# Expert stage: normalised rows stored k-major, and the slot table turned round between the two down steps

## The chip, the cores and the metric

The kernel runs on one core of one Trainium2 chip. The metric is the device time of one execution in microseconds (us); the times below are medians of a few executions. The engines are named as in the profile: PE is TensorE (PEld its weight loads), DVE is VectorE, ACT is ScalarE, POOL is GpSimd, SP is SyncE, which here only issues DMAs.

## The reference, cut to what matters

Two transformer blocks over 256 tokens of width 2048. The change touches only the mixture of experts in the first one, and the normalised rows that feed it:

```python
def hierarchical_moe(hn, w_router_group, w_router_expert, w_gate, w_up, w_down):
    """hn: (B,S,D). Top-1 group, then top-2 experts in that group; SwiGLU experts."""
    ...
    ids = g_idx * EXPERTS_PER_GROUP + top_i
    comb = jnp.sum(jax.nn.one_hot(ids, N_EXPERTS, dtype=jnp.float32) * weights[..., None], axis=1)
    out = jnp.zeros((b * s, d), jnp.float32)
    for e in range(N_EXPERTS):
        hid = jax.nn.silu(t @ w_gate[e]) * (t @ w_up[e])
        out = out + (hid @ w_down[e]).astype(jnp.float32) * comb[:, e:e + 1]
```

There are 32 experts with a hidden width of 256. All weights are float32, so the expert stage has to read 32 x 3 x 2048 x 256 x 4 bytes, 201 MB.

## The kernel before

Everything is written engine by engine, with semaphores by hand; the order on each engine is the order of the code.

**Rows.** POOL multiplies the normalised rows `hs` by the gain `g_row` and writes `xs` (L532, one instruction for each of the two token tiles of 128). ACT copies `xs` to `x_hi` in TensorE's rounded format (L1334), DVE makes `x_lo = xs - x_hi` (L1886). Behind these stand, on ACT the copy of the router's logits `lgT` (L1336), on DVE the whole routing, which ends with the one-hot slot table `G` (token by 64 slots for each expert, L1964), and on PE the product for `w_ple_up` and the ranks of the tokens.

**Gather.** The experts are worked off in 16 pairs. A gather (L901) makes two of the 16 k-tiles of the transposed rows `xg` for two pairs at once: 8 matmuls of 128x128 weights, which are columns of `x_hi` or `x_lo`, by 256 columns of `g_quad`, a copy of a piece of `G`. Feature number q*16 + k is row q of k-tile k, because the expert weights are read as `"e (p k) n -> e p (k n)"` so that each partition reads one piece of memory. So the weights of a gather are every 16th element of a row, 64 bytes apart, by the view `x_k` at L589. Eight gathers run ahead of the stage, and four in each of the pairs 0 to 13.

**One pair g.** PE runs `gate_up(g, 0..3)` (L951, into `ps`), `transpose(g)`, `down(g, 0..1)` (L973, into `acc`), and four `move(g, q)` between them. A move is a scatter of pair g-1, a gather and a second scatter. A scatter (L913, L914) brings the results `yh`, `yl` of pair g-1 back to the token rows by the turned slot table `GT`; DVE adds them to `h` (L2003). `transpose(g)` turns the hidden rows `hid` (L922) into the left half of a buffer `tp` and the pair's part of `G` (L924) into its right half; ACT copies the halves to `hid_t` (L1380) and `GT` (L1381) and then frees the buffer.

**Buffers.** All of moves and transposes go through two `tp` buffers in turn (`use`, L887): a use waits on `t_read[b]` until ACT or DVE has read the use before the last one.

**Weights.** SP loads them in 6 steps for each pair, each of 2 MB in two or four DMAs, into a ring of 4 steps (`load_step`, L413); a step's DMAs are issued when PE has used the step four before.

**Overflow.** Tokens beyond an expert's 64 slots are handled by a branch after the stage (`xT`, `ov_w`), which no instruction of the profile shows as run.

Of the kernel before, what the change touches and what calls it, by code (L numbers as in the profile page):

```python
# [27 lines left out]
P = 128  # L28
# [72 lines left out]
def program(nc, I, out):  # L101
    ctx = ExitStack()
    with ctx:
# [199 lines left out]
        silu_ready, hid_ready, hid_lo = sem("silu_ready"), sem("hid_ready"), sem("hid_lo")  # L303
# [29 lines left out]
        def _(sp):  # L333
# [60 lines left out]
            wg = I["w_expert_gate"][0].rearrange("e (ko p) n -> p (e ko) n", p=P)  # L394
            wu = I["w_expert_up"][0].rearrange("e (ko p) n -> p (e ko) n", p=P)
# [36 lines left out]
            with sp.If(count > 0):  # L432
                with sp.Fori(0, count) as i:
                    ex = sp.value_load(over_i[0:1, bass.ds(i + 1, 1)], min_val=0, max_val=N_EXPERTS - 1)
                    sp.wait_ge(ov_pe, i * OV_PE + OV_X)
                    sp.dma_start(ov_w[:, :, :], wg[:, bass.ds(ex * KT, KT), :]).then_inc(ov_in, 16)
                    sp.wait_ge(ov_pe, i * OV_PE + (OV_X + 1))
                    sp.dma_start(ov_w[:, :, :], wu[:, bass.ds(ex * KT, KT), :]).then_inc(ov_in, 16)
# [56 lines left out]
        def _(pool):  # L495
# [93 lines left out]
        x_k = [x.rearrange("p t (q k) -> p t k q", k=KT) for x in (x_hi, x_lo)]  # L589
        USES = 8 + 8 * PAIRS + 4 * (PAIRS - 2) + PAIRS + 1  # L590
# [7 lines left out]
        def _(pe):  # L598
# [285 lines left out]
            gathered = []  # L884
# [22 lines left out]
            def scatter(g, k):  # L907

                pe.wait_ge(y_ready, 2 * g + k // 4 + 1)
                o = use()  # L910
                q = slice(k % 2 * P, k % 2 * P + P)
                cs = slice(k // 2 * 512, k // 2 * 512 + 512)
                pe.matmul(o[:, :], GT[:, g % 2, q], yh[:, cs], start=True, stop=False, skip_group_check=True)  # L913
                pe.matmul(o[:, :], GT[:, g % 2, q], yl[:, cs], start=False, stop=True, skip_group_check=True).then_inc(t_done, 1)  # L914

            def transpose(g):

                pe.wait_ge(hid_ready, g + 1)
                o = use()
                hid_j = hid[:, g % 2, :].rearrange("p (q j) -> p j q", j=2)  # L920
# [35 lines left out]
            def down(g, j):  # L956
# [33 lines left out]
            for g in range(PAIRS):  # L990
# [11 lines left out]
                down(g, 0)  # L1002
                down(g, 1)
# [8 lines left out]
            with pe.If(count > 0):  # L1012
                for k in range(KT // 2):
                    if k >= 2:
                        pe.wait_ge(ov_act, k - 1)
                    for j in range(2):
                        f = slice((2 * k + j) * P, (2 * k + j + 1) * P)
                        for t in range(TT):
                            pe.matmul(tp[k % 2][:, j * S + t * P:j * S + (t + 1) * P], x_hi[:, t, f], ident_r[:, :],
                                      start=True, stop=False, skip_group_check=True)  # L1020
                            mm = pe.matmul(tp[k % 2][:, j * S + t * P:j * S + (t + 1) * P], x_lo[:, t, f], ident_r[:, :],
                                           start=False, stop=True, skip_group_check=True)
# [121 lines left out]
        def _(act):  # L1144
# [187 lines left out]
            for t in range(TT):  # L1332
                act.wait_ge(xs_ready, t + 1)
                act.activation(x_hi[:, t, :], xs[:, t, :], ACT.Copy).then_inc(xh_ready, 1)  # L1334
# [41 lines left out]
            def transposed(g):  # L1376
# [3 lines left out]
                act.activation(hid_t[:, :, :].rearrange("p a b -> p (a b)"), tp[b][:, 0:S], ACT.Copy).then_inc(hid_lo, 1)  # L1380
                act.activation(GT[:, g % 2, :], tp[b][:, S:2 * S], ACT.Copy).then_inc(t_read[b], 1)  # L1381
# [16 lines left out]
            for g in range(PAIRS):  # L1398
# [12 lines left out]
                moved(g, 3)  # L1411
                if g % 2 and g // 2 + 2 < PAIRS // 2:
# [117 lines left out]
        def _(dve):  # L1530
# [353 lines left out]
            for t in range(TT):  # L1884
                dve.wait_ge(xh_ready, t + 1)
                dve.tensor_tensor(x_lo[:, t, :], xs[:, t, :], x_hi[:, t, :], ALU.subtract).then_inc(xl_ready, 1)  # L1886
# [150 lines left out]
            for g in range(PAIRS):  # L2037
# [10 lines left out]
                moved(g, 3)  # L2048
            evict(PAIRS - 1)
# [300 lines left out]
```

## Time and profile before

| | us |
|---|---|
| three runs | 2441.45, 2442.82, 2431.88; median 2441.45 |
| the profiled execution | 2437.95 |
| its span in the trace | 2436.1 |
| PE busy | 2290.0 (94%) |
| DVE, ACT, POOL busy | 1339.8, 902.1, 25.6 |
| expert stage with its first gathers, in the span | 454.35 to about 1005 |
| PE's granted clock, mean | 0.977 of full speed |

Busy time of an engine isn't the time that it sets: what matters is which engine or transfer the others wait for in a stage. Durations are read in the stage that the change touches; matmuls are pipelined, so that the distance between starts tells more than the length of one.

### The profile page before, as it was taken

What the parts mean: (1) busy time and instruction counts of PE and PEld (TensorE: products, weight loads), DVE (VectorE), ACT (ScalarE), POOL (GpSimd) and SP (SyncE); (2) the same over time, 40 slices, a digit from 0 to 9 for tenths busy, and PEclk for the clock granted to TensorE, in tenths of its full rate; (3) what the DMA queues carried; (4) which work ended last, traced back from release to release, by engine and by line L of the source; (5) the groups of instructions that cost most, each with busy time, mean ns of one, the idle gap of its engine ahead of it and who ended that gap; (6) DMA issues with size and microseconds to landing.
All of it is one profiled execution on the core that took longest, in us unless ns stands there. A gap on an engine that the chain in (4) does not pass through costs nothing.

```text
span 2436.1 us, 31362 instructions
## 1 busy us (share of the span) xinstructions
PE 2290.0 (94%) x11443; PEld 1745.5 (72%) x11443; DVE 1339.8 (55%) x1760; ACT 902.1 (37%) x1197; POOL 25.6 (1%) x32
## 2 busy tenths in 40 slices
PE   8999789899999999898999869989999999999997
PEld 7888567654554444487888647867888888878886
DVE  7679845322222222555555557656777777764443
ACT  4464344311111111344333355444443344343332
POOL 1000000100000000000000000000000000000000
PEclk9999999999999999899999999999999999999998
DMA  8655335499999999566656505544655665556663
GB/s 286 183 161 155 104 127 194 166 358 368 374 391 372 368 363 401 208 192 215 190 190 191 155 18 160 179 128 142 187 185 186 185 185 187 183 183 195 192 194 126
DMA packets 301285, 519.26 MB, mean 213 GB/s; under 512 B 24032, under 2 KB 196096, under 8 KB 292224
## 3 DMA queue, kind: packets, MB, share of 16 engines
q1 hardware_dynamic: 298272, 505.51, 61.3%
q0 software_dynamic: 2912, 12.38, 1.5%
q8 instruction: 66, 1.08, 0.2%
q14 instruction: 35, 0.29, 0.0%
HBM read 515.67 MB, written 5.27 MB: 214 GB/s over the span
## 4 chain that ended last, share of the span: by engine, by line
PE 88%; DVE 7%; ACT 2%; issue 1%; DMA 1%; POOL 0%; DVEq 0%; SPq 0%; ACTq 0%; POOLq 0%
PE acc L610 27%; PE acc L630 24%; PE acc L631 12%; PE ps L951 9%; PE tp L901 5%; PE acc L973 5%; PE tp L913 1%; DVE rst L1838 1%; PE tp L914 1%; PE tp L686 1%; DVE wlo L1543 1%; DVE e L1702 1%; DVE sneg L1679 1%; PE tp L766 1%; DMA mw<-in_w_expert_up 1%
## 5 line engine op out<-in xcount | busy, mean ns | idle before, releaser
L630 PE MATMUL acc<-xhl,whi 128*128 128x512 f32 x2496 | 888.1, 401 | 13.9 <-DVE rxp L1595 6.5
L1159 ACT ACTIVATE whi<-raw 128x1024 fp32r<-128x1024 f32 x572 | 587.6, 1055 | 547.5 <-DMA raw<-in_w_in 186.1
L1543 DVE TENSOR_TENSOR wlo<-raw,whi 128x1024 fp32r<-128x1024 f32 x572 | 673.2, 1220 | 207.7 <-ACT whi L1159 203.9
L631 PE MATMUL acc<-xhl,wlo 128*128 128x256 f32 x2496 | 702.2, 281 | 0.0
L630 PEld LDWEIGHTS acc<-xhl,whi 128*128 128x128 f32 x2496 | 472.4, 189 | 132.0 <-DVE rxp L1595 7.2
L631 PEld LDWEIGHTS acc<-xhl,wlo 128*128 128x128 f32 x2496 | 474.5, 190 | 0.1
L610 PE MATMUL acc<-whi,xhl 128*128 128x512 f32 x1248 | 400.1, 397 | 13.5 <-DVE wlo L1543 10.3
L610 PEld LDWEIGHTS acc<-whi,xhl 128*128 128x128 f32 x1248 | 236.3, 189 | 68.0 <-DVE wlo L1543 13.2
L610 PE MATMUL acc<-wlo,xhl 128*128 128x512 f32 x624 | 244.7, 392 | 0.0
L951 PE MATMUL ps<-mw,xg 128*64 128x512 f32 x1024 | 229.8, 595 | 1.6 <-DMA mw<-in_w_expert_up 0.9
L2003 DVE TENSOR_TENSOR h<-tp,h 128x512 f32<-128x512 f32 x128 | 87.8, 690 | 207.0 <-PE tp L914 206.4
L951 PEld LDWEIGHTS ps<-mw,xg 128*64 128x64 f32 x1024 | 70.9, 137 | 140.5 <-issue 137.7
L610 PEld LDWEIGHTS acc<-wlo,xhl 128*128 128x128 f32 x624 | 118.4, 190 | 26.5 <-issue 2.6
L610 PE MATMUL acc<-whi,ah 128*128 128x512 f32 x336 | 131.8, 392 | 4.3 <-DVE xhl L2233 4.3
L610 PE MATMUL acc<-wlo,ah 128*128 128x512 f32 x336 | 131.7, 392 | 0.0
L610 PE MATMUL acc<-whi,al 128*128 128x512 f32 x336 | 131.5, 391 | 0.0
L1364 ACT ACTIVATE xg<-tp 128x512 f32<-128x512 f32 x64 | 38.2, 597 | 246.6 <-PE tp L901 246.6
L973 PE MATMUL acc<-mw,hid_t 128*64 128x512 f32 x512 | 113.5, 596 | 0.0
L2024 DVE SCALAR_TENSOR_TENSOR yl<-acc,w_slot,yh 128x1024 fp32r<-128x1024 f32 x32 | 39.6, 1279 | 123.9 <-ACT yh L1373 123.9
L973 PEld LDWEIGHTS acc<-mw,hid_t 128*64 128x64 f32 x512 | 35.4, 137 | 69.8 <-issue 69.8
L901 PE MATMUL tp<-g_quad,x_hi 128*128 128x256 f32 x256 | 75.8, 379 | 8.0 <-ACT g_quad L1358 7.1
L901 PEld LDWEIGHTS tp<-g_quad,x_hi 128*128 128x128 f32 x256 | 68.3, 309 | 18.0 <-issue 9.6
(343 smaller groups left out, 1867.4 us busy)
## 6 DMA issues: line engine op xcount, KB each, us to landing
raw<-in_w_in SPq DMA_DIRECT2D x352, 256.0 KB, 3.0
raw<-in_w_up SPq DMA_DIRECT2D x352, 256.0 KB, 2.9
mw<-in_w_expert_gate SPq DMA_DIRECT2D x128, 512.0 KB, 7.2
mw<-in_w_expert_up SPq DMA_DIRECT2D x128, 512.0 KB, 8.1
mw<-in_w_expert_down SPq DMA_DIRECT2D x64, 1024.0 KB, 11.0
raw<-in_w_down SPq DMA_DIRECT2D x176, 256.0 KB, 3.4
raw<-in_w_out SPq DMA_DIRECT2D x128, 256.0 KB, 3.3
raw<-in_w_ple_gate SPq DMA_DIRECT2D x64, 256.0 KB, 3.5
```

Of the source, the lines that this page charges most:

```text
L610: mm = pe.matmul(o, lhsT, rhs, start=first and j == 0, stop=last and j == 2, skip_group_check=True)
L630: pe.matmul(o.rearrange("p (m n) -> p m n", m=2), wh, ahl[:, :, k, :], start=first, stop=False, skip_group_check=True)
L631: return pe.matmul(o[:, S:2 * S], wl, ahl[:, 0, k, :], start=False, stop=last, skip_group_check=True)
L686: mm = pe.transpose(tp[g % 2][:, j * S + t * P:j * S + t * P + P], src[:, t, f], ident[:, :])
L901: mm = pe.matmul(o[:, j * 2 * P:(j + 1) * 2 * P], x_k[m // TT][:, m % TT, 2 * k + j, :], g_quad[:, q % 2, m % TT, :], start=m == 0, stop=m ...
L951: mm = pe.matmul(ps[g % 2][r, :].rearrange("p (a n) -> p a n", a=2), x_e, mw[:, s0 + 2 * e:s0 + 2 * e + 2, k * 256:(k + 1) * 256], start=c ...
L973: mm = pe.matmul(acc[c][r, n5], hid_t[:, j, r], mw[:, s0 + 2 * e + c, n5], start=j == 0, stop=j == 1, skip_group_check=True)
L1159: act.activation(whi[:, m % RING, :], raw[:, m % RING, :], ACT.Copy).then_inc(hi_ready, 1)
L1364: act.activation(xg[:, q % 2, 2 * k:2 * k + 2, :].rearrange("p a b -> p (a b)"), tp[b][:, :], ACT.Copy).then_inc(t_read[b], 1)
L1543: dve.tensor_tensor(wlo[:, m % RING, :], raw[:, m % RING, :], whi[:, m % RING, :], ALU.subtract).then_inc(lo_ready, 1)
L2003: dve.tensor_tensor(hh, tp[b][:, :], hh, ALU.add).then_inc(t_read[b], 1)
L2024: dve.scalar_tensor_tensor(yl[:, cs], acc[b][:, :], w_slot[:, g:g + 1], yh[:, cs], ALU.mult, ALU.subtract).then_inc(y_ready, 1)
```

## The change

`xs`, `x_hi` and `x_lo` are stored in the order k, q: the 128 elements of one k-tile lie side by side. POOL reads as before and writes 512 bytes apart. The copies of ACT and DVE take the new shape, whole rows as before. The gather's weights are now contiguous. Since the overflow branch shares these rows, its order of features changes with them, and so do the views of its weights.

The turning of the slot table leaves `transpose(g)` and gets a function and a `tp` use of its own, `slots_back(g)`, between `down(g, 0)` and `down(g, 1)`. The semaphore `hid_lo` goes; `down(g, 0)` waits on the `t_read` of `transpose(g)`'s buffer, and the first scatter of pair g on that of `slots_back(g)`. ACT copies `GT` behind the fourth gather's `xg`.

```diff
-        xs = at("xs", 33, [P, TT, D])
-        x_lo = at("x_lo", 33, [P, TT, D], F32R)
-        x_hi = at("x_hi", 49, [P, TT, D], F32R)
+        xs = at("xs", 33, [P, TT, KT, P])
+        x_lo = at("x_lo", 33, [P, TT, KT, P], F32R)
+        x_hi = at("x_hi", 49, [P, TT, KT, P], F32R)
...
-                pool.tensor_tensor(xs[:, t, :], hs[:, t, :], g_row[:, :], ALU.mult).then_inc(xs_ready, 1)
+                pool.tensor_tensor(xs[:, t, :, :].rearrange("p k q -> p q k"), hs[:, t, :].rearrange("p (q k) -> p q k", k=KT),
+                                   g_row.rearrange("p (q k) -> p q k", k=KT), ALU.mult).then_inc(xs_ready, 1)
...
-        x_k = [x.rearrange("p t (q k) -> p t k q", k=KT) for x in (x_hi, x_lo)]
-        USES = 8 + 8 * PAIRS + 4 * (PAIRS - 2) + PAIRS + 1
+        x_k = [x_hi, x_lo]
+        USES = 8 + 8 * PAIRS + 4 * (PAIRS - 2) + 2 * PAIRS + 1
...
                 pe.wait_ge(y_ready, 2 * g + k // 4 + 1)
+                if k == 0:
+                    pe.wait_ge(t_read[back_use[g] % 2], back_use[g] // 2 + 1)
                 o = use()
...
                 for j in range(2):
-                    pe.transpose(o[:, j * P:(j + 1) * P], hid_j[:, j, :], ident[:, :])
+                    mm = pe.transpose(o[:, j * P:(j + 1) * P], hid_j[:, j, :], ident[:, :])
+                mm.then_inc(t_done, 1)
+
+            def slots_back(g):
+
+                o = use()
+                back_use.append(tu.n - 1)
                 for t in range(TT):
-                    mm = pe.matmul(o[:, S + t * P:S + (t + 1) * P], G[:, t, pair_cols(g)], ident_b[:, :], start=True,
+                    mm = pe.matmul(o[:, t * P:(t + 1) * P], G[:, t, pair_cols(g)], ident_b[:, :], start=True,
                                    stop=True, skip_group_check=True)
                 mm.then_inc(t_done, 1)
...
                 if j == 0:
-                    pe.wait_ge(hid_lo, g + 1)
+                    pe.wait_ge(t_read[hid_use[g] % 2], hid_use[g] // 2 + 1)
...
                 move(g, 3)
                 down(g, 0)
+                slots_back(g)
                 down(g, 1)
...
-                act.activation(hid_t[:, :, :].rearrange("p a b -> p (a b)"), tp[b][:, 0:S], ACT.Copy).then_inc(hid_lo, 1)
-                act.activation(GT[:, g % 2, :], tp[b][:, S:2 * S], ACT.Copy).then_inc(t_read[b], 1)
+                act.activation(hid_t[:, :, :].rearrange("p a b -> p (a b)"), tp[b][:, 0:S], ACT.Copy).then_inc(t_read[b], 1)
+                tu.n += 1
+
+            def slots_back(g):
+
+                b = tu.n % 2
+                act.wait_ge(t_done, tu.n + 1)
+                act.activation(GT[:, g % 2, :], tp[b][:, 0:S], ACT.Copy).then_inc(t_read[b], 1)
                 tu.n += 1
```

PE before, pair 1 from its transposes to the second down step (`tp0` and `tp1` are the two buffers; what a row waits for stands in brackets):

```order
L922 MATMUL tp1<-ident,hid_130 128x128 [waits t_read1,hid_ready]
L922 MATMUL tp1<-ident,hid_130 128x128
L924 MATMUL tp1<-ident_b_110,G_115 128x128 x2
L913 MATMUL tp0<-yh_127,GT_116 128x512 [waits t_read0,y_ready]
L914 MATMUL tp0<-yl_128,GT_116 128x512
L901 MATMUL tp1<-g_quad_107,x_hi_106 128x256 [waits t_read1]
...
L913 MATMUL tp0<-yh_127,GT_116 128x512 [waits t_read0,y_ready]
L914 MATMUL tp0<-yl_128,GT_116 128x512
L973 MATMUL acc0<-mw_52,hid_t_131 64x512 [waits w_in_g2,y_ready,hid_lo]
L973 MATMUL acc0<-mw_52,hid_t_131 64x512 x3
L973 MATMUL acc1<-mw_52,hid_t_131 64x512 x4
L973 MATMUL acc0<-mw_52,hid_t_131 64x512 [waits w_in_g3]
```

PE after the change, the same stretch of a pair (the line numbers are those of the changed kernel: L902 is the gather, L916 and L917 the scatter, L926 the transposes, L934 the slot table, L983 the down step):

```order
L926 MATMUL tp0<-ident,hid_130 128x128 [waits t_read0,hid_ready]
L926 MATMUL tp0<-ident,hid_130 128x128
L916 MATMUL tp1<-yh_127,GT_116 128x512 [waits t_read1,y_ready]
L917 MATMUL tp1<-yl_128,GT_116 128x512
L902 MATMUL tp0<-g_quad_107,x_hi_106 128x256 [waits t_read0]
...
L983 MATMUL acc0<-mw_52,hid_t_131 64x512 [waits w_in_g0,y_ready,t_read0]
L983 MATMUL acc0<-mw_52,hid_t_131 64x512 x3
L983 MATMUL acc1<-mw_52,hid_t_131 64x512 x4
L934 MATMUL tp0<-ident_b_110,G_115 128x128 [waits t_read0]
L934 MATMUL tp0<-ident_b_110,G_115 128x128
L983 MATMUL acc0<-mw_52,hid_t_131 64x512 [waits w_in_g1]
```

The two matmuls of the slot table moved from between the transposes and a scatter into the middle of the down steps, and wait there for a buffer.

ACT before, from the third gather of a pair to the results `yh` of the same pair:

```order
L1364 ACTIVATE xg_54<-tp0 128x512 [waits t_done]
L1380 ACTIVATE hid_t_131<-tp0 128x256 [waits t_done]
L1381 ACTIVATE GT_116<-tp0 128x256
L1364 ACTIVATE xg_54<-tp0 128x512 [waits t_done]
L1373 ACTIVATE yh_127<-acc0,w_slot_122 128x1024 [waits w_used,w_ready]
```

and after:

```order
L1374 ACTIVATE xg_54<-tp0 128x512 [waits t_done]
L1390 ACTIVATE hid_t_131<-tp0 128x256 [waits t_done]
L1374 ACTIVATE xg_54<-tp0 128x512 [waits t_done]
L1397 ACTIVATE GT_116<-tp0 128x256 [waits t_done]
L1383 ACTIVATE yh_127<-acc0,w_slot_122 128x1024 [waits w_used,w_ready]
```

The copy of `GT` went behind the fourth gather's copy and has a wait of its own; on DVE nothing moves.

## Rows read from the trace of the kernel before

**Rows 1.** Windows: us, busy of PE, PEld, DVE, ACT, POOL, granted clock, DMA share, GB/s.
```profile
450.00:460.00 10.00, 5.66 (x25) 5.69 (x26) 5.87 (x16) 2.35 (x4) 0.00 (x0) 0.66 0.93 373
...
500.00:940.00 440.00, 435.02 (x1938) 216.69 (x1936) 108.38 (x143) 75.75 (x124) 0.00 (x0) 1.00 0.95 375
945.00:996.00 51.00, 47.66 (x206) 17.09 (x202) 13.63 (x20) 5.29 (x10) 0.00 (x0) 1.00 1.02 410
```

**Rows 2.** The line of the gather: duration ns min/median/max, first and last start.
```profile
L901 PEld LDWEIGHTS tp<-g_quad,x_hi x256: 291/314/331, 454.3 to 931.0; 128*128 128x128 f32 x128
```

**Rows 3.** Timeline, router product, contiguous weights: start us, us, engine line op, count.
```profile
430.66 0.39 PE L610 MATMUL ps<-xhl,rt_hi 128*128 128x256 f32 x2
...
433.12 0.28 PE L610 MATMUL ps<-xhl,rt_hi 128*128 128x256 f32 x1
...
430.77 0.19 PEld L610 LDWEIGHTS ps<-xhl,rt_lo 128*128 128x128 f32 x1
```

**Rows 4.** Timeline, end of pair 7: third move, transposes, fourth move.
```profile
723.51 0.19 PEld L913 LDWEIGHTS tp<-yh,GT 128*128 128x128 f32 x1 [0.81 <-issue]
...
724.08 0.50 PE L901 MATMUL tp<-g_quad,x_hi 128*128 128x256 f32 x2
724.38 0.68 DVE L2003 TENSOR_TENSOR h<-tp,h 128x512 f32<-128x512 f32 x1
...
725.75 0.39 PE L913 MATMUL tp<-yh,GT 128*128 128x512 f32 x1
...
726.41 0.69 DVE L2003 TENSOR_TENSOR h<-tp,h 128x512 f32<-128x512 f32 x1 [1.34 <-PE tp L914]
726.69 0.47 PE L922 MATMUL tp<-ident,hid 128*128 128x128 f32 x2 [0.32 <-ACT xg L1364]
727.00 0.27 PE L924 MATMUL tp<-ident_b,G 128*128 128x128 bf16 x2
727.25 0.47 PE L913 MATMUL tp<-yh,GT 128*128 128x512 f32 x1
...
728.02 0.51 PEld L901 LDWEIGHTS tp<-g_quad,x_hi 128*128 128x128 f32 x2 [0.51 <-ACT GT L1381]
...
729.90 0.40 PE L913 MATMUL tp<-yh,GT 128*128 128x512 f32 x1
...
730.47 0.65 PE L973 MATMUL acc<-mw,hid_t 128*64 128x512 f32 x2
```

**Rows 5.** Timeline, second move of pair 7, PE and DVE.
```profile
717.70 0.50 PE L901 MATMUL tp<-g_quad,x_hi 128*128 128x256 f32 x2
717.90 0.69 DVE L2003 TENSOR_TENSOR h<-tp,h 128x512 f32<-128x512 f32 x1 [3.56 <-PE tp L914]
...
719.36 0.40 PE L913 MATMUL tp<-yh,GT 128*128 128x512 f32 x1
```

**Rows 6.** The chain of waits ahead of the stage, in order of time: start us, us, what.
```profile
423.50 10.02 POOL xs L532 x2
433.54 1.91 ACT x_hi L1334
...
454.35 14.55 PE tp L901 x64
```

**Rows 7.** Timeline, matmuls of the first gathers.
```profile
454.93 0.66 PE L901 MATMUL tp<-g_quad,x_lo 128*128 128x256 f32 x2
...
458.06 0.60 PE L901 MATMUL tp<-g_quad,x_hi 128*128 128x256 f32 x2
...
459.40 0.61 PE L901 MATMUL tp<-g_quad,x_lo 128*128 128x256 f32 x2
```

**Rows 8.** Timeline of the loads of a step and of PE in pair 15.
```profile
473.31 4.26 SPq L413 DMA_DIRECT2D mw<-in_w_expert_down  x4
...
975.27 3.65 PE L951 MATMUL ps<-mw,xg 128*64 128x512 f32 x16 [0.34 <-DMA mw<-in_w_expert_up]
980.37 3.65 PE L951 MATMUL ps<-mw,xg 128*64 128x512 f32 x16 [0.32 <-DMA mw<-in_w_expert_up]
```

More of the change, by code:

```diff
@@ L302, in program @@
                                                                  ("rt_in", "rt_split", "rt_mm", "rt_copy", "rt_tp", "rt_read", "rt_e"))
-        silu_ready, hid_ready, hid_lo = sem("silu_ready"), sem("hid_ready"), sem("hid_lo")
+        silu_ready, hid_ready = sem("silu_ready"), sem("hid_ready")
         moe_in, xs_ready, xh_ready, xl_ready, quad_ready = (sem(n) for n in (
@@ L392, in _ @@
                 load(k2(w_pu, 0, slice(c * 512, c * 512 + 512)))
-            wg = I["w_expert_gate"][0].rearrange("e (ko p) n -> p (e ko) n", p=P)
-            wu = I["w_expert_up"][0].rearrange("e (ko p) n -> p (e ko) n", p=P)
+            wg = I["w_expert_gate"][0].rearrange("e (p k) n -> p e (k n)", p=P)
+            wu = I["w_expert_up"][0].rearrange("e (p k) n -> p e (k n)", p=P)
             wd = I["w_expert_down"][0].rearrange("e (ko p) n -> p (e ko) n", p=P)
@@ L435, in _ @@
                     sp.wait_ge(ov_pe, i * OV_PE + OV_X)
-                    sp.dma_start(ov_w[:, :, :], wg[:, bass.ds(ex * KT, KT), :]).then_inc(ov_in, 16)
+                    sp.dma_start(ov_w.rearrange("p a b -> p (a b)").unsqueeze(1), wg[:, bass.ds(ex, 1), :]).then_inc(ov_in, 16)
                     sp.wait_ge(ov_pe, i * OV_PE + (OV_X + 1))
-                    sp.dma_start(ov_w[:, :, :], wu[:, bass.ds(ex * KT, KT), :]).then_inc(ov_in, 16)
+                    sp.dma_start(ov_w.rearrange("p a b -> p (a b)").unsqueeze(1), wu[:, bass.ds(ex, 1), :]).then_inc(ov_in, 16)
                     sp.wait_ge(ov_pe, i * OV_PE + (OV_X + 2))
@@ L883, in _ @@
             tu = Count()
-            gathered = []
+            gathered, hid_use, back_use = [], [], []
             def use():
@@ L919, in transpose @@
                 o = use()
+                hid_use.append(tu.n - 1)
                 hid_j = hid[:, g % 2, :].rearrange("p (q j) -> p j q", j=2)
                 for j in range(2):
-                    pe.transpose(o[:, j * P:(j + 1) * P], hid_j[:, j, :], ident[:, :])
+                    mm = pe.transpose(o[:, j * P:(j + 1) * P], hid_j[:, j, :], ident[:, :])
[3 more added lines that the diff above has]
+                back_use.append(tu.n - 1)
                 for t in range(TT):
-                    mm = pe.matmul(o[:, S + t * P:S + (t + 1) * P], G[:, t, pair_cols(g)], ident_b[:, :], start=True,
+                    mm = pe.matmul(o[:, t * P:(t + 1) * P], G[:, t, pair_cols(g)], ident_b[:, :], start=True,
                                    stop=True, skip_group_check=True)
@@ L1016, in _ @@
                     for j in range(2):
-                        f = slice((2 * k + j) * P, (2 * k + j + 1) * P)
                         for t in range(TT):
-                            pe.matmul(tp[k % 2][:, j * S + t * P:j * S + (t + 1) * P], x_hi[:, t, f], ident_r[:, :],
+                            pe.matmul(tp[k % 2][:, j * S + t * P:j * S + (t + 1) * P], x_hi[:, t, 2 * k + j, :], ident_r[:, :],
                                       start=True, stop=False, skip_group_check=True)
-                            mm = pe.matmul(tp[k % 2][:, j * S + t * P:j * S + (t + 1) * P], x_lo[:, t, f], ident_r[:, :],
+                            mm = pe.matmul(tp[k % 2][:, j * S + t * P:j * S + (t + 1) * P], x_lo[:, t, 2 * k + j, :], ident_r[:, :],
                                            start=False, stop=True, skip_group_check=True)
@@ L1333, in _ @@
                 act.wait_ge(xs_ready, t + 1)
-                act.activation(x_hi[:, t, :], xs[:, t, :], ACT.Copy).then_inc(xh_ready, 1)
+                act.activation(x_hi[:, t, :, :], xs[:, t, :, :], ACT.Copy).then_inc(xh_ready, 1)
             act.wait_ge(rt_mm, 1)
@@ L1411, in _ @@
                 moved(g, 3)
+                slots_back(g)
                 if g % 2 and g // 2 + 2 < PAIRS // 2:
@@ L1885, in _ @@
                 dve.wait_ge(xh_ready, t + 1)
-                dve.tensor_tensor(x_lo[:, t, :], xs[:, t, :], x_hi[:, t, :], ALU.subtract).then_inc(xl_ready, 1)
+                dve.tensor_tensor(x_lo[:, t, :, :], xs[:, t, :, :], x_hi[:, t, :, :], ALU.subtract).then_inc(xl_ready, 1)
             dve.wait_ge(rt_tp, 1)
@@ L2048, in _ @@
                 moved(g, 3)
+                tu.n += 1
             evict(PAIRS - 1)
```

## The prediction, made before the changed kernel ran

> **What bounds the kernel now.** I read four views, in this order. The windows of the expert stage say that PE is busy for 435.0 of 440 us at full granted clock, and that the DMA engines are busy for 0.95 of it as well [rows 1]. So PE sets the pace of the pairs 1 to 13, but the DMA follows closely. A pair needs 12.58 MB, and at the 375 GB/s of that window this is 33.55 us a pair; in the trace the same row returns every 33.63 us. In a stretch where the DMA is never idle it moves 410 GB/s [rows 1], which is 5.11 us for a step of 2.1 MB and 30.7 us for a pair: no change to PE can bring a pair below that. Next, the gather's line against another product with the same shape. The gather's weight load takes a median of 314 ns [rows 2]; the router's, which also loads 128x128 float32 but from contiguous memory, takes 190 ns [rows 3]. What counts is the distance between starts: six gather matmuls take 1.34 us from 458.06 to 459.40, 0.223 us each [rows 7], the router's 21 matmuls from 430.66 to 433.12 take 0.117 us each [rows 3], with the same 256 moving columns. So the gather is paced by its weight loads and the router by its columns. Third, the timeline of the moves shows who waits for whom around the gathers [rows 4, 5]. Last, the chain of waits ahead of the stage: POOL's two products, ACT's copy and then PE stand in it one behind the other [rows 6].
>
> **The storage order: the gathers.** The only thing about the gather's matmuls that changes is the distance of the weight elements, 64 bytes before and 4 after. I price it by the router's row, which differs in nothing that the rows show: a matmul falls from 0.223 to 0.117 us, and a gather of eight from 1.66 us (717.70 to 719.36, [rows 5]) to 0.94 us. The other bound is no gain at all (a rival below).
>
> How much of the 0.72 us reaches the end is decided by the two buffers. The second scatter of a move writes the buffer of the first, so it waits until DVE has read that one. In the second move DVE reads until 718.59, 0.89 us after the gather's start, and a handover from DVE to PE takes some 0.12 us (727.10 to the weight load ahead of 727.25, [rows 4]): 1.01 us, a little more than the shorter gather. Now DVE is early and hidden behind the gather; it will be late by 0.07 us. So the first and the second move gain 1.66 - 1.01 = 0.65 us each.
>
> The third move, the transposes and the fourth move go together, since a wait in one eats what the one before gained [rows 4]. First scatter at 723.51 as now; gather from 724.08 to 725.02. DVE reads that scatter late, until 725.06, as it made `hid` first; second scatter at 725.18 instead of 725.75. The transposes follow the gather's end by ACT's copy, 0.94 us (725.75 to 726.69): 725.96. The fourth move's first scatter needs DVE's read of the scatter before, 1.50 us after that one's start (725.75 to 727.25): 726.68. That is later than the end of the transposes even without the slot table, so taking the table's two matmuls (0.27 us) out of there gains nothing by itself: the wait on DVE takes their place. Gather 0.57 us later, at 727.25; second scatter 1.01 us behind it, 728.26; down step 0.57 us behind that (729.90 to 730.47), at 728.83. It starts at 730.47 now: gain 1.64 us. The 0.51 us in which the fourth gather waits for ACT's `GT` copy is in this sum; it goes, as `hid_t` alone is read long before 727.25.
>
> **The slot table's new place.** Two bf16 matmuls, 0.27 us, between down steps that use half the array each. The buffer is free: ACT has read the fourth gather's `xg` while `down(g, 0)` runs for 3.5 us. Changing between half and full array costs too. Bounds: 0.27 us, and 0.27 + 0.81 us, the idle time of the weight load at the nearest such change [rows 4], most of which lies beside running matmuls. I take 0.5 us. The second down step, SP's release of its ring slot and ACT's `yh` wait behind it, by 0.5 us. ACT's `GT` copy (0.38 us) lies beside the second down step and is needed 10 us later. The first scatter's new wait is met by then.
>
> A pair gains 2 x 0.65 + 1.64 - 0.5 = 2.44 us, and the 13 pairs with four gathers and scatters 31.7 us. Their new period is 31.2 us, 0.5 us above the DMA's 30.7.
>
> **First gathers, pairs 0, 14, 15.** The first eight gathers, 64 matmuls, take 14.55 us on the chain [rows 6]. PE was idle ahead of them, and the granted clock is 0.66 of full over 450 to 460 us [rows 1], the lower level at first: rows start 0.45 us apart from 454.93 on and last 0.66 us, at 458.06 they last 0.60 [rows 7]. At half clock 256 columns take about twice the router's 0.117 us, so the first 15 matmuls gain nothing. The other 49 gain 0.106 us each, 5.2 us. ACT's copies of 0.6 us keep up with a gather in 0.94. Pair 0 has four gathers without scatters, the last behind many small matmuls; I count three at 0.85 us less 0.5 for the slot table, 2.0 us. Pairs 14 and 15 have no gathers, pay 0.5 and get back the wait for `GT`: 0.
>
> **The storage order: POOL.** POOL's two products are 10.02 us of the chain [rows 6]: x_hi, the logits, the ranks and the slot table all wait behind them, and what they grow by, the kernel grows by. They read as before and write 512 bytes apart. No row has a strided write on POOL. Bounds: 0, if reading two operands sets its pace, and +10 us, if a strided write doubles it (the nearest row of a stride is PE's load, 314 against 190 ns, 1.65 times, which would be +6.5). I take 0, since only one of three operands changed, and keep +10 for the range. ACT's and DVE's passes over the rows stay whole and contiguous: 0.
>
> On this the Trainium skill speaks against the change. GPSIMD Engine Reference, "Performance pitfalls for Q7 kernels", says that reading with a step above 8 bytes costs about half more per element; it says nothing on writes. If writes paid the same, the sum would be 5 us worse, about 2406. No row here shows it.
>
> **DMA.** With pairs of 31.2 us the DMA is busy for 0.98 of the time and its lead is thinner when pairs 14 and 15, which PE does in some 27 us, come. Already now pair 15 waits for weights, 0.3 us at a time [rows 8]. I count 2 us (0 to 6). In all, the ring's first slot comes free at about 468 (473.31 [rows 8] less 5.2), and 92 steps of 5.11 us end near 940, before PE's own last down step at about 956, so the floor isn't reached as a whole.
>
> HBM Reference, "Specifications (TRN2)", gives a core 358 GB/s when both cores of a pair stream and about 425 alone. By 358 the stage would be bound by the DMA today and gain nothing; by 425 the 2 us would go. The rows, 375 over 440 us and 410 over 51 us, speak for the second.
>
> **Sum.** 5.2 + 2.0 + 31.7 - 2 = 36.9 us off the profiled execution's 2437.95 (span 2436.1 and 1.9 around it): 2401. That execution lies between the three runs, 3.5 us below their median and 6 above the lowest, so 2401 stands for a middling run.
>
> **Rivals.** (a) *The DMA becomes the bound.* If, when loaded without a break, it keeps only what the long window implies, 375 / 0.95 = 395 GB/s, a pair takes 31.9 us instead of 31.2: 9 us for 13 pairs, and some 2 more at the end, 2412. For it: its share is at 0.95 already. Against it: 410 over 51 us. (b) *POOL's strided write is late*: +5 to +10 us, 2406 to 2411. (c) *The loads aren't slow because of the stride*, so the change doesn't do what it says: the gathers stay, 16 x 0.5 us come on, up to 0.5 us of `GT` waits for each pair go: 2437 to 2446, taken 2442. Against it: the router's loads. (d) *Slower*: POOL writes each element of the strided output on its own. From a pass of 29.5 us instead of 5.0 on (14 ns an element against 2.4 now) the gain is gone and 12 us lost: 2450 and more. Only the lack of any row speaks for it. (e) Handovers shrink more than I count, or the slot table costs 0.3: 2391.
>
> **How the numbers follow.** Forecast (2394 to 2407) 0.59, (a) 0.13, (b) 0.17, (c) 0.05, (d) 0.02, (e) 0.04. The likeliest gives 2401. The range 2391 to 2413 takes in the forecast, (a), (b) and (e) and leaves out (c), (d) and the ends of the spread. A measurement of this kernel can tell about 0.5% (12 us) from no change. Faster by more than that: 0.93; within: 0.05, from (c) and the far end of (b); slower: 0.02, from (d).
>
> **What would show it.** The gather's weight load near 190 ns and its matmuls 0.117 us apart; moves one and two with the second scatter released by DVE; a pair every 31.2 us; the first gathers done in about 9.4 us; POOL's two products still 10 us; DMA share near 0.98, and PE's waits for weights below 10 us in all. Weight loads still at 314 ns would make the prediction wrong by its whole size; PE waiting for weights in every pair would speak for (a); a longer POOL row for (b).

## The result, and the profile after

| | us |
|---|---|
| after, four runs | median 2396.57 (2394.19 to 2399.26) |
| before, four runs | median 2436.66 (2431.79 to 2442.82) |
| after / before | 0.983, 95% interval 0.980 to 0.987 |
| the profiled execution after | 2394.19, its span 2392.4 |
| forecast | 2401, range 2391 to 2413 |

The change saves 40 us of the medians, 1.7%, and 43.8 us between the two profiled executions. The forecast was 4 us too high. Line numbers are those of the changed kernel from here on: L902 is the gather, L916 and L917 the scatter, L926 the transposes, L934 the slot table, L961 gate_up, L983 the down step, and DVE's addition to `h` is L2020.

First the stage as a whole, to be laid beside [rows 1]. The windows of the kernel after, with the same columns:

```profile
450.00:460.00 10.00, 5.95 (x37) 5.98 (x38) 5.58 (x16) 3.28 (x6) 0.00 (x0) 0.66 0.92 356
500.00:900.00 400.00, 394.57 (x1890) 175.40 (x1888) 105.96 (x141) 74.64 (x121) 0.00 (x0) 1.00 1.01 402
```

In 400 us PE is still busy for 394.6 us, but the DMA share has risen from 0.95 to 1.01 and the rate from 377 (the kernel before over the same 400 us; 375 over the 440 us of [rows 1]) to 402 GB/s. Next, the gather's line (duration in ns min/median/max, first and last start), the answer to [rows 2]:

```profile
L902 PEld LDWEIGHTS tp<-g_quad,x_hi x256: 186/188/338, 454.0 to 894.2; 128*128 128x128 f32 x128
L902 PE MATMUL tp<-g_quad,x_hi x256: 274/282/582, 454.1 to 894.3; 128*128 128x256 f32 x128
```

The weight load fell from 314 to 188 ns, that of the router's contiguous load [rows 3]. The chain of waits ahead of the stage, as in [rows 6], and the line of POOL's products in full:

```profile
423.16 10.07 POOL xs L532 x2
433.25 1.91 ACT x_hi L1344
...
454.05 9.40 PE tp L902 x64
```

```profile
L532 POOL TENSOR_TENSOR xs<-hs,g_row x2: 4627/5051/5475, 423.2 to 428.6; 128x2048 f32<-128x2048 f32 x2
```

POOL writes 512 bytes apart and takes 10.07 us for both products, against 10.02 before. The first gathers take 9.40 us instead of 14.55 (in other executions with the same loads 9.4 to 10.1, by how long the lower clock lasts). Their timeline shows the two clock levels, the answer to [rows 7]:

```profile
456.75 0.63 PE L902 MATMUL tp<-g_quad,x_hi 128*128 128x256 f32 x2
...
457.55 0.40 PE L902 MATMUL tp<-g_quad,x_hi 128*128 128x256 f32 x2
457.79 0.40 PE L902 MATMUL tp<-g_quad,x_lo 128*128 128x256 f32 x2
```

Rows of two start 0.43 us apart until 457.18, which is the lower clock, and 0.24 us apart from 457.55 on, 0.12 us a matmul.

Last, the timeline of one pair, the second move and then the stretch of [rows 4]:

```profile
695.83 0.50 PE L916 MATMUL tp<-yh,GT 128*128 128x512 f32 x1
...
696.41 0.40 PE L902 MATMUL tp<-g_quad,x_hi 128*128 128x256 f32 x2
...
696.61 0.69 DVE L2020 TENSOR_TENSOR h<-tp,h 128x512 f32<-128x512 f32 x1 [3.57 <-PE tp L917]
...
697.42 0.19 PEld L916 LDWEIGHTS tp<-yh,GT 128*128 128x128 f32 x1
697.45 0.47 PE L916 MATMUL tp<-yh,GT 128*128 128x512 f32 x1
...
698.08 3.65 PE L961 MATMUL ps<-mw,xg 128*64 128x512 f32 x16
...
701.67 0.50 PE L916 MATMUL tp<-yh,GT 128*128 128x512 f32 x1
...
704.13 0.48 PE L926 MATMUL tp<-ident,hid 128*128 128x128 f32 x2
...
704.95 0.47 PE L916 MATMUL tp<-yh,GT 128*128 128x512 f32 x1 [0.34 <-DVE h L2020]
...
705.49 0.39 PE L902 MATMUL tp<-g_quad,x_hi 128*128 128x256 f32 x2
...
706.53 0.47 PE L916 MATMUL tp<-yh,GT 128*128 128x512 f32 x1
...
707.15 3.65 PE L983 MATMUL acc<-mw,hid_t 128*64 128x512 f32 x16
...
710.73 0.11 PEld L934 LDWEIGHTS tp<-ident_b,G 128*128 128x128 bf16 x2 [0.81 <-issue]
...
710.95 3.65 PE L983 MATMUL acc<-mw,hid_t 128*64 128x512 f32 x16
...
714.44 1.03 PE L961 MATMUL ps<-mw,xg 128*64 128x512 f32 x4
```

By the spacing of its matmuls the gather is over at about 697.36, and DVE's read ends at 697.30; the second scatter starts at 697.45, 1.04 us after the gather's start (forecast 1.01). In the fourth move the first scatter waits for DVE, as forecast. To measure the same stretches before, four more rows of the kernel before are wanted: the start of the second move, the weight load of its second scatter and the gate_up behind it (around [rows 5]), and the gate_up behind the down steps of [rows 4]:

```profile
717.12 0.50 PE L913 MATMUL tp<-yh,GT 128*128 128x512 f32 x1
...
719.23 0.20 PEld L913 LDWEIGHTS tp<-yh,GT 128*128 128x128 f32 x1
...
719.92 3.65 PE L951 MATMUL ps<-mw,xg 128*64 128x512 f32 x16
...
737.39 3.17 PE L951 MATMUL ps<-mw,xg 128*64 128x512 f32 x14
```

The move took 2.80 us and takes 2.25 now (695.83 to 698.08). The two down steps took 6.92 us (730.47 [rows 4] to 737.39) and take 7.29 with the slot table in between (707.15 to 714.44).

What the stage gained in all is read further down: the second group of transposes in the code behind it (L686 before, L687 after, in the chain that ended last) starts at 980.91 instead of 1018.46, 37.55 us earlier. The forecast's sum was 36.9.

### The profile page after: what moved, and what is told of

Same layout as the page of the kernel before. It is cut to its first block, busy times and chain, and to the rows that moved or that the text cites. A ratio compares the mean times of both kernels' runs of the same rounds, so it can differ in the third digit from the quotient of the medians.

```text
span 2392.4 us, 31362 instructions
## 1 busy us (share of the span) xinstructions
PE 2245.1 (94%) x11443; PEld 1697.4 (71%) x11443; DVE 1340.0 (56%) x1760; ACT 904.3 (38%) x1197; POOL 25.7 (1%) x32
## 4 chain that ended last, share of the span: by engine, by line
PE 89%; DVE 7%; ACT 2%; issue 1%; DMA 1%; POOL 0%; DVEq 0%; SPq 0%; ACTq 0%; POOLq 0%
PE acc L611 27%; PE acc L631 25%; PE acc L632 13%; PE ps L961 9%; PE acc L983 5%; PE tp L902 3%; PE tp L916 2%; PE tp L917 1%; DVE rst L1855 1%; PE tp L687 1%; DVE e L1719 1%; DVE sneg L1696 1%; PE tp L767 1%; DVE h L2020 1%; DVE wlo L1560 1%
## 5 line engine op out<-in xcount | busy, mean ns | idle before, releaser
L961 PE MATMUL ps<-mw,xg 128*64 128x512 f32 x1024 | 229.7, 595 | 1.4 <-issue 0.7
L2020 DVE TENSOR_TENSOR h<-tp,h 128x512 f32<-128x512 f32 x128 | 87.6, 690 | 171.9 <-PE tp L917 171.9
L961 PEld LDWEIGHTS ps<-mw,xg 128*64 128x64 f32 x1024 | 70.9, 137 | 140.2 <-issue 137.5
L983 PE MATMUL acc<-mw,hid_t 128*64 128x512 f32 x512 | 117.6, 601 | 0.0
L983 PEld LDWEIGHTS acc<-mw,hid_t 128*64 128x64 f32 x512 | 34.1, 137 | 62.6 <-issue 61.0
L1521 ACT ACTIVATE ah<-af 128x512 f32 (+1 forms) x21 | 13.3, 632 | 170.5 <-DVE af L2249 170.5
L611 PEld LDWEIGHTS acc<-whi,ah 128*128 128x128 f32 x336 | 63.5, 189 | 17.8 <-DVE xhl L2251 4.6
```

Of the source, the lines that this page charges most:

```text
L611: mm = pe.matmul(o, lhsT, rhs, start=first and j == 0, stop=last and j == 2, skip_group_check=True)
L961: mm = pe.matmul(ps[g % 2][r, :].rearrange("p (a n) -> p a n", a=2), x_e, mw[:, s0 + 2 * e:s0 + 2 * e + 2, k * 256:(k + 1) * 256], start=c ...
L983: mm = pe.matmul(acc[c][r, n5], hid_t[:, j, r], mw[:, s0 + 2 * e + c, n5], start=j == 0, stop=j == 1, skip_group_check=True)
L2020: dve.tensor_tensor(hh, tp[b][:, :], hh, ALU.add).then_inc(t_read[b], 1)
```

## The experiments

A good measure of the stage is the period: the distance between the transposes of neighbouring pairs in the timeline, which repeats within 0.07 us through pairs 1 to 13 in every kernel but e10_short_gate; the table has its mean. The one beside it is the time from the transposes of pair 0 to those of pair 15. Total times of single executions scatter by some 15 us (17 runs of the kernel before, beside the first four kernels: 2426.32 to 2441.64), too much for terms of 5 us; the periods don't.

| kernel | time, us | period | pair 0 to 15 | DMA share, GB/s, 500 to 900 |
|---|---|---|---|---|
| before | 2436.66 | 33.64 | 493.6 | 0.95, 377 |
| after | 2396.57 | 31.38 | 464.7 | 1.01, 402 |
| after_again | 2397.03 | 31.38 | 464.7 | 1.01, 402 |
| e1_order_alone | 2391.65 | 31.03 | 461.1 | 1.01, 406 |
| e2_slots_alone | 2439.48 | 33.63 | 495.2 | 0.95, 377 |
| e7_slots_in_ps | 2388.19 | 31.01 | 459.8 | 1.01, 406 |
| e3_stride8 | 2411.15 (one run) | 31.38 | 465.8 | 1.01, 402 |
| e4_stride16 | 2438.87 (one run) | 33.96 | 499.9 | 0.94, 371 |
| e5_half_gather | 2395.68 (one run) | 31.38 | 462.9 | 1.01, 402 |
| e8_pool_read_strided | 2398.46 (one run) | 31.38 | 465.3 | 1.01, 402 |
| e10_short_gate | 2375.96 (one run) | 30.45 | 453.3 | 1.02, 413 |
| e11_short_gate_half_load | 2345.82 (one run) | 27.57 | 406.6 | 0.70, 233 |

### Which half of the change carries the gain

The kernel after once more, on the chip of the next three:

> The changed kernel again, on the same chip as the three beside it, as their yardstick. Both theories: 2396 us or so, a pair of experts every 31.4 us (33.6 before), PE waiting for weights only in pair 15.

It gave 2397.03 us (five runs), 0.985 of the kernel before (0.982 to 0.987), and the same period.

Then the storage order alone: `transpose(g)` keeps the slot table and the semaphore `hid_lo`, as in the kernel before.

```diff
             def transpose(g):
...
-                    mm = pe.transpose(o[:, j * P:(j + 1) * P], hid_j[:, j, :], ident[:, :])
-                mm.then_inc(t_done, 1)
+                    pe.transpose(o[:, j * P:(j + 1) * P], hid_j[:, j, :], ident[:, :])
+                for t in range(TT):
+                    mm = pe.matmul(o[:, S + t * P:S + (t + 1) * P], G[:, t, pair_cols(g)], ident_b[:, :], start=True,
...
-                slots_back(g)
                 down(g, 1)
```

> Only the storage order k, q; the slot table is turned round inside the transposes as in the kernel before. Theory A (the whole gain is the contiguous weight load; moving the slot table costs its two changes between half and full array): the transposes plus the slot table's two matmuls end just before DVE frees the buffer for the next scatter, and the GT copy ends when the shortened fourth gather can start, so the old place costs nothing now; a pair takes 31.43 - 0.37 = 31.06 us, and the run is 5 us FASTER than the full change. Theory B (the GT copy ahead of the fourth gather still holds PE, as it did for 0.5 us): a pair takes some 31.6 us, 3 to 7 us slower than the full change. Theory C (the DMA sets the pace at 31.4 us a pair): same as the full change, with PE waiting for weights.

It ran in 2391.65 us, 0.983 of before (0.981 to 0.985), and the pairs come every 31.03 us, 0.35 us sooner than with the whole change. Its waits (engine, line, waited for: us in total, times, longest):

```profile
PE tp L914 <- DVE h L2003: 3.7, 14, 0.7
...
PEld tp L902 <- ACT GT L1381: 3.2, 13, 0.3
```

L914 and L1381 are the scatter and the copy of `GT` there. In the fourth move of pair 7, L925 being the slot table:

```profile
700.12 0.28 PE L925 MATMUL tp<-ident_b,G 128*128 128x128 bf16 x2
...
700.62 0.47 PE L914 MATMUL tp<-yh,GT 128*128 128x512 f32 x1 [0.23 <-DVE h L2003]
...
701.14 0.30 PEld L902 LDWEIGHTS tp<-g_quad,x_hi 128*128 128x128 f32 x2 [0.25 <-ACT GT L1381]
701.16 0.48 PE L902 MATMUL tp<-g_quad,x_hi 128*128 128x256 f32 x2
```

The slot table's two matmuls are over at 700.40, and the first scatter waits for DVE until 700.62, so they lie inside that wait. The gather's weight load still waits 0.25 us for the copy of `GT`, instead of 0.51, but beside the scatter's matmuls: the gather starts 0.54 us behind the scatter, exactly as in the kernel after (704.95 to 705.49), where nothing waits for `GT` at that place. So the table costs nothing in its old place once the gathers are short. This is theory A.

The slot table alone, with the rows stored as before (shown against the kernel after):

```diff
-        x_k = [x_hi, x_lo]
+        x_k = [x.rearrange("p t (q k) -> p t k q", k=KT) for x in (x_hi, x_lo)]
...
-                pool.tensor_tensor(xs[:, t, :, :].rearrange("p k q -> p q k"), hs[:, t, :].rearrange("p (q k) -> p q k", k=KT),
-                                   g_row.rearrange("p (q k) -> p q k", k=KT), ALU.mult).then_inc(xs_ready, 1)
+                pool.tensor_tensor(xs[:, t, :], hs[:, t, :], g_row[:, :], ALU.mult).then_inc(xs_ready, 1)
...
```

> Only the slot table's new place and buffer; the rows are stored q, k as before and the weight loads stay at 314 ns. Theory A: the 0.27 us that leave the transposes are replaced by the wait for DVE, 0.25 us of the GT wait are gained and 0.37 us are paid in the down steps: 33.7 to 33.8 us a pair, 0 to 3 us slower than before. Theory B (the wait for GT and the slot table's matmuls were both on the path): 33.2 us a pair, 5 us faster than before.

2439.48 us, 1.001 of before (0.999 to 1.003): no difference. The period is 33.63 us: the `GT` wait that it removes and the price of the new place cancel. From the third move to the down step a pair takes 6.58 us there (724.28 to 730.86) against 6.96, 0.38 less, and the table costs 0.37 in the down steps; theory A had 0.25 for the first. Its pairs 0 to 15 are 1.6 us longer. Between pair 0 and pair 1 it is 2.1 us (34.87 against 32.74), and there the lower clock lasts longer: the granted clock over 490 to 500 us is 0.66 against 0.83 in the kernel before, and the first down step, 3.5 us at full clock, is slow:

```profile
493.60 5.55 PE L982 MATMUL acc<-mw,hid_t 128*64 128x512 f32 x16
```

A third place, half of a `ps` buffer, in the old order: the table's matmuls stand right behind the transposes but need no `tp` buffer, so that `hid_t` alone holds it.

```diff
             def slots_back(g):
 
-                o = use()
-                back_use.append(tu.n - 1)
+                o = ps[(g + 1) % 2]
...
-                mm.then_inc(t_done, 1)
+                mm.then_inc(gt_mm, 1)
...
+                slots_back(g)
...
                 down(g, 0)
-                slots_back(g)
                 down(g, 1)
```

> The full change, but the slot table is turned round right behind the transposes into the ps bank that is idle in this pair, so that it needs neither a use of the two tp buffers nor a change of the array in the down steps, and PE does it while it waits for DVE. Theory A: a pair takes 31.43 - 0.37 = 31.06 us, 5 to 6 us faster than the full change, same as the storage order alone. Theory C (DMA sets the pace): same time as the full change, PE's waits for weights grow by 5 us.

2388.19 us (six runs), 0.983 of before (0.980 to 0.987), with the period of e1, 31.01 us; no gather waits for `GT` any more, and nothing was won by that. The gather starts 0.54 us behind the scatter here too, and the wait on DVE stays:

```profile
PE tp L917 <- DVE h L2020: 3.3, 14, 0.3
```

By whole times e1 and e7 can't be told from the kernel after with certainty, nor from each other; from pair 0 to pair 15 they are 3.6 and 4.9 us faster. (e1 gives back 1.3 of its gain ahead of pair 15, where it waits for weights.) e7 has the shortest median and the shortest pairs.

### How far apart may the weights lie

The rows stored in groups of two k-tiles, so that the elements of a weight column lie 8 bytes apart, and in groups of four, 16 bytes apart. POOL writes in that order, the views of the overflow branch follow, and everything else is the kernel after. The edit for 8 bytes (for 16, `KT // 4` and `4`):

```diff
-        x_hi = at("x_hi", 49, [P, TT, KT, P], F32R)
+        x_hi = at("x_hi", 49, [P, TT, KT // 2, P, 2], F32R)
...
-                        mm = pe.matmul(o[:, j * 2 * P:(j + 1) * 2 * P], x_k[m // TT][:, m % TT, 2 * k + j, :], g_quad[:, q % 2, m % TT, :],
+                        mm = pe.matmul(o[:, j * 2 * P:(j + 1) * 2 * P], x_k[m // TT][:, m % TT, (2 * k + j) // 2, :, (2 * k + j) % 2], g_quad[:, q % 2, m % TT, :],
```

> The full change with rows stored in the order k/2, q, k%2: the gather's weights lie 8 bytes apart instead of 4. Theory A (each weight load slows with the distance at once): the transposes of hid, whose weights also lie 8 bytes apart, load in 206 ns, so about 205 to 210 ns a load, and the matmuls stay 0.117 to 0.125 us apart. Theory B (distances within 16 bytes cost nothing, as SBUF - State Buffer of the Trainium skill has it in its part on cachelines, four float32 apart for free): 190 ns, 0.117 us apart. In both, the run stays within 5 us of the full change; the trace decides.

> The same with the order k/4, q, k%4: weights 16 bytes apart. Theory A (cost by the step in memory up to 64 bytes): a load between 210 and 314 ns, say 250, matmuls about 0.16 us apart, a pair of experts 0.5 to 1 us longer than with contiguous weights. Theory B (only steps beyond 16 bytes cost): 190 ns and 0.117 us, no difference. Theory C (every load that opens a new 16-byte line for each element pays in full): 314 ns and 0.223 us apart, as before the change, and the whole gain of the order is gone.

The gather's weight loads of the two, 8 bytes first:

```profile
L903 PEld LDWEIGHTS tp<-g_quad,x_hi x256: 192/195/332, 456.6 to 897.6; 128*128 128x128 f32 x128
```

```profile
L903 PEld LDWEIGHTS tp<-g_quad,x_hi x256: 307/329/337, 454.1 to 937.4; 128*128 128x128 f32 x128
L903 PE MATMUL tp<-g_quad,x_hi x256: 281/396/603, 454.2 to 937.6; 128*128 128x256 f32 x128
```

At 8 bytes a load takes 195 ns, between the two theories, and the period is 31.38 us, that of the kernel after. At 16 bytes it takes 329 ns, the matmuls start 0.233 us apart, and the period is 33.96 us, worse than the kernel before by 0.32. That is theory C: the whole gain of the order is gone. So the distance is the cause, almost the whole price comes at one step between 8 and 16 bytes, and at 64 bytes it isn't higher: 314 ns [rows 2]. Why 16 bytes cost 15 ns more than 64 stays open. The whole time of e3, 2411.15, came from an execution whose stage was as short as that of the kernel after; what it was longer by lies outside the pairs. The Trainium skill ("Advanced Engine Details and Errata", "SBUF Cachelines") speaks of lines of 16 bytes that want two hits each. 8 bytes of distance give two hits, 16 give one, so these two runs agree with it. The figure that the expectation took from SBUF — State Buffer of the Trainium skill, four float32 apart for free, doesn't hold here: that is just the distance of 16 bytes, and it pays in full.

### What sets the moves now

Half of each gather left out, the matmuls with `x_lo` (its output lacks that part of every gathered row):

```diff
-                    for m in range(2 * TT):
+                    for m in range(TT):
```

> The full change with the x_lo half of each gather left out: four matmuls instead of eight, 0.47 us less of PE in each. Theory A (with contiguous weights DVE's read of the first scatter sets when the second scatter of a move may start, 1.0 us after the gather's start): a pair takes 31.3 to 31.4 us as now, PE stands idle in the moves for DVE, and only the gathers ahead of the stage and in pair 0 get shorter, some 5 us in all. Theory B (PE's own matmuls set the pace of the moves): a pair falls by 1.9 us until the DMA holds it at 30.7, some 15 us in all, with PE waiting for weights.

```profile
500.00:900.00 400.00, 369.89 (x1684) 151.26 (x1682) 105.63 (x140) 76.05 (x122) 0.00 (x0) 1.00 1.01 402
```

```profile
699.69 0.47 PE L916 MATMUL tp<-yh,GT 128*128 128x512 f32 x1 [0.65 <-DVE h L2020]
...
701.26 0.47 PE L916 MATMUL tp<-yh,GT 128*128 128x512 f32 x1 [0.41 <-DVE h L2020]
```

PE is busy for 24.7 us less in 400 and waits for DVE in each move instead. The period stays at 31.38 us, to the hundredth, as theory A had it. So with the gathers this short the second scatter of every move hangs on DVE's read of the first, and no shorter gather can bring more. From the first gathers to the transposes of pair 1 the kernel gains 6.1 us (theory A: 5); its whole time, in one run, is only 0.9 below the median of the kernel after. In the waits of the kernel after this limit hardly shows:

```profile
PE tp L916 <- DVE h L2020: 4.4, 13, 0.3
```

These are the first scatters of the fourth moves alone; at the second scatters gather and read end within 0.1 us of each other, and two limits of the same length hide one another.

### POOL: reading or writing with a stride

The same product, written contiguously and read with 64 bytes of distance, so that the element order in memory is the same:

```diff
-                pool.tensor_tensor(xs[:, t, :, :].rearrange("p k q -> p q k"), hs[:, t, :].rearrange("p (q k) -> p q k", k=KT),
-                                   g_row.rearrange("p (q k) -> p q k", k=KT), ALU.mult).then_inc(xs_ready, 1)
+                pool.tensor_tensor(xs[:, t, :, :], hs[:, t, :].rearrange("p (q k) -> p k q", k=KT),
+                                   g_row.rearrange("p (q k) -> p k q", k=KT), ALU.mult).then_inc(xs_ready, 1)
```

> The full change, but POOL walks xs in the order in which it lies and reads hs and g_row 64 bytes apart, instead of reading in order and writing 512 bytes apart (5.05 us a pass, 5.02 with everything contiguous). Theory A (reading sets POOL's pace): each pass gets longer by half, as GPSIMD Engine Reference of the Trainium skill says of reads with a step above 8 bytes, 7.5 us, and the kernel by 5 us, since the passes stand in the chain ahead of the stage. Theory B (POOL is bound by its own instructions for an element): 5.05 us as now, no difference.

```profile
L532 POOL TENSOR_TENSOR xs<-hs,g_row x2: 7238/7792/8345, 421.6 to 429.8; 128x2048 f32<-128x2048 f32 x2
```

```profile
460.56 10.06 PE tp L902 x64
```

Reading with a stride takes 7.79 us for a product instead of 5.05, 54% more, and the first gathers start at 460.56 instead of 454.05 although the products began 1.6 us earlier. 5.5 us of that are POOL's. PE's product for `w_ple_up` on the same chain was 2.4 us longer in this execution, at a lower clock: PE had been idle for 7.51 us ahead of it (1.76 in the kernel after), the granted clock was 0.50 over 440 to 445 us (1.00), and its first matmuls started 0.43 us apart instead of 0.23. That the longer idle time brought this about isn't shown, since after_again has 0.70 over 435 to 440 us with POOL as fast as ever. The 7 us stay through pair 0, whose transposes start at 491.31 instead of 484.15; the whole time of this one run is 1.9 above the median of the kernel after, where theory A had 5, and single runs scatter by more. Writing 512 bytes apart is free here (5.05 against 5.02). The Trainium skill's figure for reads (GPSIMD Engine Reference, "Performance pitfalls for Q7 kernels": about half more) agrees with this run. It says nothing on writes, and the prediction was right not to carry it over to them.

### Is the DMA the next bound

A quarter of gate_up's matmuls left out (one k-tile in four of each step), in the kernel e7, with all bytes still loaded; the output lacks those k-tiles.

```diff
-                for k in range(4):
+                for k in range(3):
```

> The slot table turned into a half of its own PSUM place as in e7 (pairs about 30.9 us), and 3 of the 4 k-tiles of each gate and up product left out of TensorE's work, a quarter of its matmuls, while every byte of the weights is still loaded. The output is not the reference's. Four gate_up calls of 3.65 us lose about 0.9 us each, so TensorE alone would need some 27.5 us a pair. Theory D (the DMA is the next bound, at 410 GB/s, 30.7 us a pair): the pairs come every 30.7 us and not faster, DMA share stays at 1.0 to 1.02 and 402 to 410 GB/s in the window from 500 to 900, and TensorE waits for weights some 3 us in each pair. Rival: the DMA still has room when asked (the share over 1.0 is an artefact of its counting), pairs fall to 28 to 29 us and the rate rises to 430 GB/s and more.

And the same with half the bytes of each tile from the fifth load step on, so that its weights are wrong as well:

```diff
+                n_el = m * CHUNK if step < STEP else m * CHUNK // 2
...
-                    sp.dma_start(dst, w[e, :, m * c * CHUNK:m * (c + 1) * CHUNK]).then_inc(w_in_g[r], 16)
+                    sp.dma_start(dst, w[e, :, m * c * CHUNK:m * c * CHUNK + n_el]).then_inc(w_in_g[r], 16)
```

> As e10, and from the fifth load step on only half of the bytes of each weight tile are loaded. The output is not the reference's. Theory D: with the bytes halved TensorE never waits for weights, and the pairs come every 27.5 to 28.5 us. If the period of e10 was set by something else (DVE's reads of the moves, which are late now in every pair), it stays at e10's period although the DMA is at half load.

The windows and one wait of e10, then the windows of e11:

```profile
500.00:900.00 400.00, 368.35 (x1722) 165.18 (x1722) 109.62 (x145) 74.65 (x122) 0.00 (x0) 0.98 1.02 413
```

```profile
704.00 2.80 PE L963 MATMUL ps<-mw,xg 128*64 128x512 f32 x12 [2.23 <-DMA mw<-in_w_expert_up]
```

```profile
500.00:900.00 400.00, 394.42 (x1892) 179.39 (x1890) 121.89 (x163) 79.94 (x132) 0.00 (x0) 1.00 0.70 233
```

With a quarter of gate_up gone PE waits for weights in many steps, the pairs come unevenly (29.0 to 33.0 us apart) and 30.45 us on the mean of pairs 1 to 13. 12.58 MB in 30.45 us are 413 GB/s. With half the bytes the wait is gone and the period falls to 27.57 us, PE's own. So in e10 the DMA sets the pace, and its floor is 30.5 us a pair, 0.9 us below the kernel after and 0.6 below e1 and e7. The prediction took 30.7 and said that no change to PE could bring a pair below that; e10 is 0.25 below it.

The share of 1.01 in the kernel after looks like a bound that is reached, and isn't: at the same share e1 still moved 406 GB/s, and e10 moved 413 at 1.02. PE's waits for weights tell it, and they are 0.7 us in two places in the kernel after, both in pair 15.

## Why the prediction was right, by its steps

**The gathers.** Load 188 ns, matmuls 0.12 us apart, first gathers 9.40 us against the 9.4 forecast, a gain of 5.15 (5.2 forecast). That these agree so well is in part luck: the same 64 matmuls took 10.01 us in after_again, where the lower clock lasted longer. The reason given, the distance of the weights, holds by e3 and e4; rival (c) is out.

**The moves.** The first and the second were forecast at 0.65 us each. The second measures 0.55. Two parts of the term were mis-sized: the second scatter starts 1.04 us behind the gather instead of 1.01, as the prediction read the handover (0.12 us) up to the scatter's weight load and not to its matmul. And it now takes 0.63 us from it to gate_up instead of 0.56: its weight load started 0.13 us ahead of its matmul, behind the gather (719.23 and 719.36), and now starts 0.03 us ahead of it (697.42 and 697.45). The block from the third move to the down step takes 5.48 us (701.67 to 707.15) against 6.96, a gain of 1.48 instead of 1.64, for the same two reasons; the second strikes twice there, since DVE's read of the third move's second scatter comes later by it too. The claim behind the sum, that DVE's read is what comes next, is shown by e5.

**The slot table.** 0.37 us (7.29 against 6.92) instead of 0.5, inside the bounds. What was said of its old place, that a wait on DVE takes it over, is shown by e1 and e7: it gains nothing to leave it. The prediction let the 0.51 us in which the fourth gather waits for `GT` go by the move of the table; e1 shows that they go with the short gathers alone. Taken together this half of the change costs 0.35 us a pair, 4.6 us in the 13 pairs. The prediction never priced the new order with the table left in place, and so didn't see that the change would be better without this half.

**The period.** 2 x 0.55 + 1.48 - 0.37 = 2.21 us by these rows and 2.26 by the periods, against 2.44 forecast: 29.4 us for 13 pairs instead of 31.7.

**Pair 0 and pairs 14, 15.** The next pair's gate_up starts 7.18 us earlier (494.76 against 501.94), 1.74 of it won in pair 0, forecast 2.0. Its other three gathers gain 0.82 to 0.86 us each (0.85 forecast). Its fourth, which the sum left out, runs behind the small matmuls at the lower clock, 0.215 us apart (484.81 to 486.82 for its eight and the handover, 2.09 us before), so it gains next to nothing. Its two down steps take 0.86 us more than before (7.94 against 7.08), not 0.5: the lower clock reaches further into them. Pairs 14 and 15, forecast at 0, are shorter by some 0.4 and 0.2 us each by their transposes.

**DMA.** The 2 us were wrong: they didn't come. Pair 15 waits for weights as before, 0.3 us at a time: 0.7 us in all against 0.9. The nearness of the floor was right, and rival (a) out: in e10 the DMA gives 413 GB/s over 400 us, not 395.

**POOL.** 0, as taken, on the ground that only one of three operands changed. e8 bears out that reads pay; that writes don't is seen in the kernel after (10.07 us against 10.02). Before the run nothing bore on writes, so that it came out at 0 and not at +5 or more was a guess that held.

**The sum.** The terms came to 36.9 us and the stage gave 37.5: 0.3 from an earlier start (454.05 against 454.35), 5.15 from the first gathers, 1.7 in pair 0, 29.4 in pairs 1 to 13, 0.6 in the last two and 0.4 unassigned. This is nearer than the terms deserve, and partly luck: the pairs 1 to 13 were counted 2.3 us too high, and the 2 us taken off for the DMA didn't come. The whole span fell by 43.7 us, 6.2 more. These 6.2 lie behind the stage, where the same code takes different times from one execution to the next: from the second group of transposes to the end of the span it is 1417.6 us before and 1411.5 after, but 1421.3 in after_again, the same kernel as after. A window of the second block's feed-forward part, before and then after:

```profile
1704.00:2156.00 452.00, 452.00 (x2560) 391.98 (x2560) 337.78 (x401) 183.82 (x201) 0.00 (x0) 1.00 0.60 186
```

```profile
1670.00:2114.00 444.00, 444.00 (x2563) 388.28 (x2563) 337.99 (x401) 184.40 (x202) 0.00 (x0) 1.00 0.61 189
```

Nearly the same number of matmuls takes 8 us less at the same granted clock, while two stretches ahead of it (1106 to 1565 before, 1068.5 to 1533.5 after) took 6 us more. The medians differ by 40.1 us, between the two.

## What to carry to other kernels

Look at PE's weight loads of the same shape in different places. The one that took 1.65 times as long here read its weights 64 bytes apart, and the engine that wrote the operand could take over the order at no cost: POOL, on its output side. Before removing a step from a path, look whether a wait of the same length lies beside it: here the slot table's old place was free and the new one cost 4.6 us. When a load is made shorter, price what it hid, too (handovers, the weight load of the next instruction), and measure a stage by its period, not by the time of the whole kernel.

## What the runs showed of the hardware that was not expected

- The price of a distance between weights was a step, not a slope: 188 ns at 4 bytes, 195 at 8, 329 at 16, 314 at 64, for 128x128 float32.
- POOL's product of 128x2048 float32 takes 5.05 us written 512 bytes apart, 5.02 written contiguously, and 7.79 read 64 bytes apart.
- A DMA share of 1.01 at 402 GB/s left room for 413.
- In the same code 2560 matmuls took 452 us in one execution and 2563 took 444 in another, both at a granted clock of 1.00. The cause stays open.
